# Packing a 96-token expert down product into column groups: 64 latent tokens on two groups of 64, 32 context tokens on four groups of 32

## The chip, the cores and the metric

The kernel runs on one core of one Trainium2 chip. The metric is device time in microseconds (us) of one launch; lower is better. TensorE multiplies a stationary operand (up to 128 rows by 128 columns, loaded by a weight load) with a moving operand that streams through it, and accumulates in PSUM, a memory of 128 partitions in 8 banks. All data are 32-bit floats, and each matmul of the program shows in the trace as two records with a weight load each.

## The reference

Two layers act on 256 context tokens and 512 latent tokens of width 1024. Each has a token mixer (four branches) and then a mixture of 16 experts, in which each expert chooses its tokens. Only the experts matter here:

```python
def ec_moe(h, w_router, w_e_gate, w_e_up, w_e_down):
    b, t, d = h.shape
    cap = EC_CAPACITY * t // N_EXPERTS
    aff = jax.nn.softmax((h @ w_router).astype(jnp.float32), axis=-1)
    vals, idx = lax.top_k(jnp.swapaxes(aff, 1, 2), cap)
    xs = jax.vmap(lambda hb, ib: hb[ib])(h, idx)
    hid = jax.nn.silu(jnp.einsum('becd,edf->becf', xs, w_e_gate)) * jnp.einsum('becd,edf->becf', xs, w_e_up)
    ys = jnp.einsum('becf,efd->becd', hid, w_e_down) * vals[..., None].astype(h.dtype)
    return jax.vmap(lambda yb, ib: jnp.zeros((t, d), yb.dtype).at[ib.reshape(-1)].add(yb.reshape(-1, d)))(ys, idx)
```

Latent and context tokens are chosen apart: an expert takes 64 latent tokens, and in the first layer also 32 context tokens (the second layer's context output isn't needed). The hidden width is 1408 (11 blocks of 128).

## The kernel before

Each engine has a program of its own; semaphores order them. `moe(L)` on each engine runs the expert stage of layer L as a loop over 16 experts (15 in the loop, the last one after it). `cap` is 96 in the first layer and 64 in the second; `two` is true in the second layer only.

*Weights.* SP streams an expert's weights in nine pieces of at most 2 MiB through three slots of the tile `ring`: gate 0, up 0, gate 1, up 1, gate 2, up 2 (the last two 384 columns wide, 1.5 MiB), then three pieces of the down weights (4, 4 and 3 blocks of 128 rows). A slot is refilled (`freed`, `piece`, issues at L2314 and L2319) when TensorE has used the piece that lies in it, so a piece is asked for three pieces ahead.

*TensorE, for each expert.* `gate_up(0)`; `choose()` for the next expert (L959, and L963 in the second layer): products of a 0/1 selection `e_sel` with the token numbers and affinities `e_ta`, which give the next expert's row offsets and scales; `gate_up(1)`; `gate_up(2)`; `turn_rows()` (L972), which transposes the next expert's gathered rows; then `down(0)`, `down(1)`, `down(2)` (L1026), which begin after the previous expert's results have been taken out of PSUM (`ys_a`, `ys_d`). In the first layer `gate_up` (L999) makes the hidden values in transposed form, 64 weight columns on each of two column groups and the 96 tokens moving. `down` has the tokens' hidden values `e_hidT` stationary and the down weights moving: two matmuls of 512 columns for each of the 11 blocks k. In the second layer the two halves of the output go to PSUM partitions 0 to 63 and 64 to 127, so that each uses its own group of 64 columns of the array. In the first layer all 96 tokens are stationary, and both halves write partitions 0 to 95.

```python
for half in range(2):
    lo = 64 * half if two else 0
    ins = pe.matmul(banks[6 + half][lo:lo + cap, :], e_hidT[:, at, 0:cap], w[:, k, half * 512:half * 512 + 512],
                    start=(f == 0), stop=(f == NF - 1))
```

*The others.* ScalarE takes out the first output half (times the affinity, from `s_sel`) into `e_ys`, VectorE the second (L1535). GpSimd then scatters `e_ys` into the rows `f_rows` in memory (`scatter`, L2198), adding, and before that gathers the next expert's rows (`gather`, L2189) with the offsets `idx` that VectorE copies from what `choose` made (`next_chosen`, `now_chosen`, L1540).

Elsewhere, the modulation product `ada_rows` (L537) puts block k on column group k mod 4, with 32 stationary columns each.

Of the kernel before, what the change touches and what calls it, by code (L numbers as in the profile page):

```python
# [19 lines left out]
ALU = mybir.AluOpType  # L20
AF = mybir.ActivationFunctionType
AX = mybir.AxisListType
P = 128
# [5 lines left out]
NT = T // P  # L29
# [127 lines left out]
def hybrid_layers(nc, I, out, stop=None):  # L157
    ctx = ExitStack()
    with ctx:
# [266 lines left out]
        s_pc = small[:, 492:504].rearrange("p (i t) -> p i t", i=2)  # L426
        s_mrow = area(WORK_W - 1024, 1024).rearrange("p (b n) -> p b n", b=2)
        s_l = small[:, 512:640]
        s_sel = small[:, 504:506]

        def parts(n, cap):

# [14 lines left out]
        def _(pe):  # L447
# [486 lines left out]
            def moe(L):  # L934
# [20 lines left out]
                def choose():  # L955

                    pe.wait_ge(sems["sel"], c.nth("sel"))
                    for t in QT:
                        ins = pe.matmul(banks[5][0:cap, 0:2], e_sel[:, t, 0:cap], e_ta[:, t, :], start=(t == QT[0]), stop=(t == QT[-1]))  # L959
                    if two:  # L960

                        for t in QT:
                            ins = pe.matmul(banks[5][64:64 + cap, 0:2], e_sel[:, t, 0:cap], e_ta[:, t, :],  # L963
                                            start=(t == QT[0]), stop=(t == QT[-1]))
                    ins.then_inc(sems["chosen"], 1)

                def turn_rows():
# [8 lines left out]
                def expert(e, last):  # L976
                    def wpiece(i):
                        n = n0 + i
                        pe.wait_ge(sems[f"w_in{n % SLOTS}"], (e * 3 + (n // SLOTS + 1)) * 16)

                    def gate_up(g):

                        for u in range(2):
                            wpiece(2 * g + u)
                            n = EXP_W[2 * g + u]
                            w = slot(n0 + 2 * g + u, n)
                            for k in range(KD if two else 0):

                                b = banks[(0, 2, 0)[g] + u]
                                pe.matmul(b[0:64, 0:256], e_xs[:, k, 0:64], w[:, k, 0:256], start=(k == 0), stop=(k == KD - 1))  # L990
                                ins = pe.matmul(b[64:128, 0:n - 256], e_xs[:, k, 0:64], w[:, k, 256:n],  # L991
                                                start=(k == 0), stop=(k == KD - 1))
                            for f in range(0 if two else n // P):

                                b = banks[(0, 2, 0)[g] + u]
                                for k in range(KD):
                                    for half in range(2):
                                        lo, c0 = 64 * half, f * P + 64 * half
                                        ins = pe.matmul(b[lo:lo + 64, f * cap:(f + 1) * cap], w[:, k, c0:c0 + 64], e_xs[:, k, 0:cap],  # L999
                                                        start=(k == 0), stop=(k == KD - 1))  # L1000
                            ins.then_inc(sems["gu"], 1)

                    def turn_hidden(g):

                        pe.wait_ge(sems["hid"], c.nth("hid"))
                        pe.nop(nofuse=True)
                        b = banks[(4, 5, 4)[g]]
                        for j in range(2 if two else 0):

                            rows = P if 4 * g + 2 + j < NF else 64  # L1010
                            ins = pe.transpose(b[:, j * P:j * P + rows], e_hid[0:rows, 512 * g + j * P:512 * g + (j + 1) * P],
                                               ident[0:rows, 0:rows])
                        ins.then_inc(sems["hid_t"], 1)

                    def down(i):
                        if two or i == 2:
                            pe.wait_ge(sems["hid_f"], c.nth("hid_f"))
                        wpiece(6 + i)
                        kk = EXP_DOWN[i]
                        w = slot(n0 + 6 + i, 1024, kk)  # L1020
                        for k in range(kk):
                            f = 4 * i + k
                            at = 4 * i + ((0, 2, 1, 3)[k] if two else k)
                            for half in range(2):
                                lo = 64 * half if two else 0
                                ins = pe.matmul(banks[6 + half][lo:lo + cap, :], e_hidT[:, at, 0:cap], w[:, k, half * 512:half * 512 + 512],  # L1026
                                                start=(f == 0), stop=(f == NF - 1))
                        ins.then_inc(sems["ys"], 1)

                    pe.wait_ge(sems["xs"], c.nth("xs"))  # L1030
                    gate_up(0)
                    if not last:
                        choose()
                    gate_up(1)
                    if two:
                        turn_hidden(0)
                    else:
                        pe.wait_ge(sems["hid_f"], c.nth("hid_f"))
                    gate_up(2)
                    if not last:  # L1040

                        pe.wait_ge(sems["idx_next"], c.nth("idx_next"))
                    if two:
                        turn_hidden(1)
                    else:
                        pe.wait_ge(sems["hid_f"], c.nth("hid_f"))
                    if not last:
                        turn_rows()

                    pe.wait_ge(sems["ys_a"], c.nth("ys_a"))  # L1050
                    pe.wait_ge(sems["ys_d"], c.nth("ys_d"))
                    down(0)
                    if two:
                        turn_hidden(2)
                    down(1)
                    down(2)

# [45 lines left out]
        def _(act):  # L1103
# [3 lines left out]
            def do(*a, **kw):  # L1107
                c.seq(act.activation(*a, **kw))  # L1108
# [318 lines left out]
            def moe(L):  # L1427
# [23 lines left out]
                def expert():  # L1451
                    hidden(0)
                    hidden(1)
                    if cap == 64:
                        turned(0)
                    hidden(2)
                    if cap == 64:
                        turned(1)
                        turned(2)

                    act.wait_ge(sems["idx_now"], c.nth("idx_now"))
                    act.wait_ge(sems["ys"], c.nth("ys", 3))
                    do(e_ys[0:cap, 0:512], banks[6][0:cap, :], AF.Copy, scale=s_sel[0:cap, 1:2])
                    act.sem_inc(sems["ys_a"], 1)

                act.sem_inc(sems["ys_a"], 1)
                per = {"gu": 6, "idx_now": 1, "ys": 3, "act_order": 4 + 4 * (cap == 64)} | ({"hid_t": 3} if cap == 64 else {})
                with act.Fori(0, NE) as e:
                    c.begin(e, per)
                    expert()  # L1470
# [51 lines left out]
        def _(dve):  # L1522
# [16 lines left out]
            def copy(o_, a):  # L1539
                S(dve.tensor_copy(o_, a))  # L1540
# [496 lines left out]
            def moe(L):  # L2037
# [2 lines left out]
                S(dve.memset(e_sel, 0.0))  # L2040
                ts(e_ta[:, :, 0], cc("tokens"), -float(first_row[L]), ALU.add)
                cap = CAPS if len(QS) == 2 else CAP_L
                both = P if cap == 64 else cap

                def select(e):

                    copy(s_pc[:, 0, t0:NT], e_pos[:, t0:NT, bass.ds(e, 1)].squeeze(2))
# [8 lines left out]
                def next_chosen():  # L2056

                    dve.wait_ge(sems["chosen"], c.nth("chosen"))
                    copy(idx[0:cap, 0:1], banks[5][0:cap, 0:1])
                    copy(s_sel[0:both, 0:1], banks[5][0:both, 1:2])  # L2060
                    dve.sem_inc(sems["idx_next"], 1)

                def now_chosen():
                    copy(idx[0:cap, 1:2], idx[0:cap, 0:1])
                    copy(s_sel[0:both, 1:2], s_sel[0:both, 0:1])
                    dve.sem_inc(sems["idx_now"], 1)

                def tokens():
# [28 lines left out]
                def expert(e, last):  # L2097
                    if not last:
                        select(e + 1)
                    hidden(0)  # L2100
                    dve.wait_ge(sems["put"], c.nth("put"))
                    now_chosen()
                    if not last:
                        next_chosen()
                    hidden(1)
                    hidden(2)
                    if not last:
                        tokens()
                    dve.wait_ge(sems["ys"], c.nth("ys", 3))
                    ts(e_ys[0:cap, 512:1024], banks[7][both - cap:both, :], s_sel[both - cap:both, 1:2], ALU.mult)  # L2110
                    dve.sem_inc(sems["ys_d"], 1)

                select(0)
# [1 line left out]
                tokens()  # L2115
                dve.sem_inc(sems["ys_d"], 1)
                per = {"silu": 3, "gu": 6, "chosen": 1, "rows_t": 1, "ys": 3, "put": 1,
                       "dve_order": 2 + len(QS) + 2 + 3 + (cap == 64) + 3 * len(QS) + 1 + 2}
                with dve.Fori(0, NE - 1) as e:
                    c.begin(e, per)  # L2120
                    expert(e, False)
# [360 lines left out]
```

## Time and profile before

| | |
|---|---|
| median of 3 runs | 3922.82 us (3918.15 to 3925.51) |
| span of the profiled execution, first to last instruction | 3927.2 us (no separate time of it was recorded) |
| first layer's expert stage | from 1341 us to about 2162 us |
| second layer's expert stage | from 3211 us to about 3900 us |
| TensorE busy in all | 3615.3 us, 92% of the span |
| mean granted TensorE clock | 0.958 of full speed |

The profile comes from one execution. PE is TensorE's matmuls, PEld its weight loads, DVE VectorE, ACT ScalarE, POOL GpSimd, SP the engine that issues the weight DMAs. Matmuls are pipelined, so a record lasts longer than the step from one to the next: steps are read from starts.

### The profile page before, as it was taken

Reading aid. Unit: us, or ns where it says so; the run is one execution under the profiler, and the core shown is the slowest. Engines: PE = TensorE matmul, PEld = TensorE weight load, DVE = VectorE, ACT = ScalarE, POOL = GpSimd, SP = SyncE. Lnnn points to the kernel's source line nnn. Section 1 sums busy time; section 2 is a strip of 40 time slices with the busy share of each in tenths; the row PEclk is TensorE's granted clock in tenths of the full one; section 3 lists DMA queues with packets and bytes.
Section 4 is the critical chain, followed back from the end, with each engine's and each line's share of the span. In section 5 each row is a group of like instructions: output and inputs, shape, how many; then the busy total and the mean of one; then the engine's idle time right before and its main releaser. Section 6 shows DMA issues by size and latency. Waiting matters only on the chain.

```text
span 3927.2 us, 63160 instructions
## 1 busy us (share of the span) xinstructions
PE 3615.3 (92%) x26440; PEld 2513.5 (64%) x26440; DVE 1091.0 (28%) x2410; ACT 702.6 (18%) x1331; POOL 127.7 (3%) x184
## 2 busy tenths in 40 slices
PE   6999999999999999999999999998989998888886
PEld 3565766767785877777777766756677664444443
DVE  0333323426612411111110452315165231111111
ACT  3322312012213000000000332221122211101101
POOL 0000100000000000000000000000000000000000
PEclk9999999999899999999999999898989999999998
DMA  5662010020102499999999202020111239999997
GB/s 203 229 227 72 22 54 22 12 75 28 56 25 85 150 348 356 354 356 348 353 356 345 90 28 71 23 75 11 54 37 61 75 150 412 412 411 414 414 410 315
DMA packets 121756, 740.26 MB, mean 188 GB/s; under 512 B 7808, under 2 KB 13952, under 8 KB 84624
## 3 DMA queue, kind: packets, MB, share of 16 engines
q1 hardware_dynamic: 110000, 695.29, 45.2%
q0 software_dynamic: 11616, 43.05, 3.8%
q8 instruction: 95, 1.56, 0.2%
q14 instruction: 45, 0.37, 0.0%
HBM read 713.09 MB, written 25.21 MB: 188 GB/s over the span
## 4 chain that ended last, share of the span: by engine, by line
PE 75%; DMA 15%; DVE 5%; ACT 3%; issue 1%; DVEq 0%; SPq 0%; POOL 0%; ACTq 0%; POOLq 0%
PE psum L566 13%; PE psum L1026 10%; PE psum L999 9%; PE psum L494 7%; DMA ring<-in_w_e_gate 6%; DMA ring<-in_w_e_down 6%; PE psum L487 5%; PE psum L471 4%; PE psum L990 4%; PE psum L892 4%; PE psum L568 3%; PE psum L656 3%; PE psum L674 2%; PE psum L761 2%; DMA ring<-in_w_e_up 2%; DVE work L1531 2%
## 5 line engine op out<-in xcount | busy, mean ns | idle before, releaser
L566 PE MATMUL psum<-HT,ring 128*128 128x256 f32 x2560 | 624.3, 400 | 17.9 <-DVEq L1607 7.8
L566 PEld LDWEIGHTS psum<-HT,ring 128*128 128x128 f32 x2560 | 509.4, 202 | 121.8 <-issue 29.2
L1026 PE MATMUL psum<-ring,work 128*96 128x512 f32 (+1 forms) x1408 | 466.3, 596 | 24.7 <-DMA ring<-in_w_e_down 24.6
L999 PE MATMUL psum<-work,ring 128*64 128x96 f32 x11264 | 474.9, 246 | 6.3 <-issue 4.2
L999 PEld LDWEIGHTS psum<-work,ring 128*64 128x64 f32 x11264 | 466.4, 137 | 21.4 <-issue 18.0
L990 PE MATMUL psum<-ring,work 128*64 128x256 f32 x1536 | 371.1, 399 | 97.8 <-DMA ring<-in_w_e_gate 73.4
L990 PEld LDWEIGHTS psum<-ring,work 128*64 128x64 f32 x1536 | 212.9, 143 | 230.7 <-DMA ring<-in_w_e_gate 89.0
L991 PE MATMUL psum<-ring,work 128*64 128x256 f32 (+1 forms) x1536 | 352.0, 369 | 0.0
L1026 PEld LDWEIGHTS psum<-ring,work 128*96 128x96 f32 (+1 forms) x1408 | 166.2, 150 | 289.7 <-issue 256.9
L494 PE MATMUL psum<-ring,HT 128*128 128x512 f32 (+1 forms) x768 | 276.0, 521 | 0.0
L1108 ACT ACTIVATE work<-psum,small 128x768 f32<-128x768 f32 (+3 forms) x176 | 131.2, 745 | 784.0 <-PE psum L1026 493.8
L494 PEld LDWEIGHTS psum<-ring,HT 128*128 128x128 f32 x768 | 145.8, 190 | 127.2 <-issue 120.5
L1111 ACT ACTIVATE work<-psum 128x512 f32<-128x512 f32 (+8 forms) x229 | 109.9, 480 | 629.9 <-PE psum L494 236.9
L487 PE MATMUL psum<-HT,ring 128*128 128x512 f32 (+5 forms) x624 | 216.0, 508 | 6.5 <-ACTq L1174 6.2
L991 PEld LDWEIGHTS psum<-ring,work 128*64 128x64 f32 x1536 | 194.9, 142 | 1.0
L1108 ACT ACTIVATE YT<-psum,pack 128x256 f32<-128x256 f32 x160 | 75.9, 474 | 616.2 <-PE psum L568 569.3
L1535 DVE TENSOR_SCALAR work<-psum,small 128x64 f32<-128x64 f32 (+3 forms) x122 | 52.9, 434 | 479.4 <-PE psum L1026 432.0
L487 PEld LDWEIGHTS psum<-HT,ring 128*128 128x128 f32 (+2 forms) x624 | 112.5, 182 | 108.1 <-issue 91.9
L1108 ACT ACTIVATE X<-psum 128x384 f32<-128x384 f32 (+3 forms) x112 | 43.4, 387 | 757.7 <-PE psum L999 420.2
L471 PE MATMUL psum<-const 128*128 128x256 f32 x732 | 170.1, 391 | 0.0
L568 PE MATMUL psum<-YT 128*128 128x256 f32 x640 | 164.3, 379 | 0.0
L471 PEld LDWEIGHTS psum<-const 128*128 128x128 f32 x732 | 142.4, 197 | 19.9
(172 smaller groups left out, 3253.2 us busy)
## 6 DMA issues: line engine op xcount, KB each, us to landing
ring<-in_w_e_gate SPq DMA_DIRECT2D x64, 2048.0 KB, 9.5
ring<-in_w_e_up SPq DMA_DIRECT2D x64, 2048.0 KB, 10.4
ring<-in_w_e_down SPq DMA_DIRECT2D x64, 2048.0 KB, 9.7
ring<-in_w_ada SPq DMA_DIRECT2D x24, 2048.0 KB, 9.5
ring<-in_w_e_gate SPq DMA_DIRECT2D x32, 1536.0 KB, 12.1
ring<-in_w_e_up SPq DMA_DIRECT2D x32, 1536.0 KB, 8.9
ring<-in_w_e_down SPq DMA_DIRECT2D x32, 1536.0 KB, 9.7
ring<-in_w_gate SPq DMA_DIRECT2D x16, 2048.0 KB, 8.9
```

The source lines that it names most:

```text
L471: pe.matmul(b[:, 0:256], ident, const[:, 0:256], start=True, stop=True)
L487: ins = pe.matmul(b[0:M, 0:n], w[:, k, c0:c0 + M], HT[:, k, off:off + n], start=(k == 0), stop=(k == KD - 1))
L494: ins = pe.matmul(b[:, 0:n], HT[:, k, t * P:(t + 1) * P], w[:, k, c0:c0 + n], start=(k == 0), stop=(k == KD - 1))
L566: pe.matmul(b[:, 0:256], w[:, k, d4 * P:(d4 + 1) * P], HT[:, k, off:off + 256], start=(k == 0), stop=(k == KD - 1))
L568: ins = pe.matmul(b[:, 256:512], wbr[:, m % 2, i, d4 * P:(d4 + 1) * P], YT[:, n_ % 2, i, off:off + 256], start=(i == 0), stop=(i == 1))
L656: ins = pe.matmul(b[:, m, at:at + ln], q(it, m), k(it, m, at, ln), start=True, stop=True)
L892: ins = pe.matmul(b[:, :], mT[:, k, t * P:(t + 1) * P], w[:, k, :], start=(k == 0), stop=(k == KD - 1))
L990: pe.matmul(b[0:64, 0:256], e_xs[:, k, 0:64], w[:, k, 0:256], start=(k == 0), stop=(k == KD - 1))
L991: ins = pe.matmul(b[64:128, 0:n - 256], e_xs[:, k, 0:64], w[:, k, 256:n], start=(k == 0), stop=(k == KD - 1))
L999: ins = pe.matmul(b[lo:lo + 64, f * cap:(f + 1) * cap], w[:, k, c0:c0 + 64], e_xs[:, k, 0:cap], start=(k == 0), stop=(k == KD - 1))
L1026: ins = pe.matmul(banks[6 + half][lo:lo + cap, :], e_hidT[:, at, 0:cap], w[:, k, half * 512:half * 512 + 512], start=(f == 0), stop=(f == ...
L1108: c.seq(act.activation(*a, **kw))
```

## The change

In the first layer the down product is made in two loops for each piece of weights. The first has the 64 latent tokens stationary, one output half on each of two 64-column groups, as the second layer does. The second has the 32 context tokens stationary, each quarter of the output (256 columns) on one of four 32-column groups, into bank 4. `choose` therefore makes offsets and scales for latent tokens on two partition ranges and for context tokens on four; `s_sel` has a column for each kind. The evictions become one of 64x512 and two of 32x256 for ScalarE and the same for VectorE. The second layer's products are the same as before, except that `choose` alternates the two groups from tile to tile (one loop in place of two).

```diff
                 def choose():
                     pe.wait_ge(sems["sel"], c.nth("sel"))
-                    for t in QT:
-                        ins = pe.matmul(banks[5][0:cap, 0:2], e_sel[:, t, 0:cap], e_ta[:, t, :], start=(t == QT[0]), stop=(t == QT[-1]))
-                    if two:
-                        for t in QT:
-                            ins = pe.matmul(banks[5][64:64 + cap, 0:2], e_sel[:, t, 0:cap], e_ta[:, t, :],
-                                            start=(t == QT[0]), stop=(t == QT[-1]))
+                    for t in range(CT, NT):
+                        for lo in (0, 64):
+                            ins = pe.matmul(banks[5][lo:lo + CAP_L, 0:2], e_sel[:, t, 0:CAP_L], e_ta[:, t, :],
+                                            start=(t == CT), stop=(t == NT - 1))
+                    for t in range(0 if two else CT):
+                        for q in range(4):
+                            ins = pe.matmul(banks[5][32 * q:32 * q + CAP_C, 2:4], e_sel[:, t, CAP_L:CAPS], e_ta[:, t, :],
+                                            start=(t == 0), stop=(t == CT - 1))
                     ins.then_inc(sems["chosen"], 1)
...
                             for half in range(2):
-                                lo = 64 * half if two else 0
-                                ins = pe.matmul(banks[6 + half][lo:lo + cap, :], e_hidT[:, at, 0:cap], w[:, k, half * 512:half * 512 + 512],
-                                                start=(f == 0), stop=(f == NF - 1))
+                                lo = 64 * half
+                                ins = pe.matmul(banks[6 + half][lo:lo + CAP_L, :], e_hidT[:, at, 0:CAP_L],
+                                                w[:, k, half * 512:half * 512 + 512], start=(f == 0), stop=(f == NF - 1))
+                        for k in range(0 if two else kk):
+                            f = 4 * i + k
+                            for q in range(4):
+                                ins = pe.matmul(banks[4][32 * q:32 * q + CAP_C, 0:256], e_hidT[:, f, CAP_L:CAPS],
+                                                w[:, k, q * 256:q * 256 + 256], start=(f == 0), stop=(f == NF - 1))
                         ins.then_inc(sems["ys"], 1)
...
-                    do(e_ys[0:cap, 0:512], banks[6][0:cap, :], AF.Copy, scale=s_sel[0:cap, 1:2])
+                    do(e_ys[0:CAP_L, 0:512], banks[6][0:CAP_L, :], AF.Copy, scale=s_sel[0:CAP_L, 1, 0:1])
+                    for q in range(2 if cap != 64 else 0):
+                        do(e_ys[CAP_L:CAPS, 256 * q:256 * q + 256], banks[4][32 * q:32 * q + CAP_C, 0:256], AF.Copy,
+                           scale=s_sel[32 * q:32 * q + CAP_C, 1, 1:2])
...
-                    copy(idx[0:cap, 0:1], banks[5][0:cap, 0:1])
-                    copy(s_sel[0:both, 0:1], banks[5][0:both, 1:2])
+                    copy(idx[0:CAP_L, 0:1], banks[5][0:CAP_L, 0:1])
+                    if cap != 64:
+                        copy(idx[CAP_L:CAPS, 0:1], banks[5][CAP_L:CAPS, 2:3])
+                        copy(s_sel[:, 0, :], banks[5][:, 0:4].rearrange("p (g c) -> p g c", g=2)[:, :, 1])
+                    else:
+                        copy(s_sel[:, 0, 0:1], banks[5][:, 1:2])
...
-                    ts(e_ys[0:cap, 512:1024], banks[7][both - cap:both, :], s_sel[both - cap:both, 1:2], ALU.mult)
+                    ts(e_ys[0:CAP_L, 512:1024], banks[7][64:64 + CAP_L, :], s_sel[64:64 + CAP_L, 1, 0:1], ALU.mult)
+                    for q in range(2, 4 if cap != 64 else 2):
+                        ts(e_ys[CAP_L:CAPS, 256 * q:256 * q + 256], banks[4][32 * q:32 * q + CAP_C, 0:256],
+                           s_sel[32 * q:32 * q + CAP_C, 1, 1:2], ALU.mult)
```

## Rows read from the trace of the kernel before

**Rows 1.** The page: its span, and DMA busy tenths in 40 slices.
```profile
span 3927.2 us, 63160 instructions
...
DMA  5662010020102499999999202020111239999997
```

**Rows 2.** Stages: us, busy us (instructions) per engine, PE clock, DMA share, GB/s.
```profile
1341.00:2145.00 804.00, 790.89 (x12233) 601.00 (x12234) 99.54 (x276) 51.80 (x78) 35.73 (x30) 1.00 0.93 350
3211.00:3900.00 689.00, 570.87 (x4233) 320.11 (x4232) 80.21 (x237) 68.82 (x143) 35.93 (x31) 0.97 0.99 404
```

**Rows 3.** Timeline of one expert, TensorE: start us, us, what, count [idle before].
```profile
1607.79 1.18 PE L959 MATMUL psum<-X 128*96 128x2 f32 x12
1608.90 18.88 PE L999 MATMUL psum<-work,ring 128*64 128x96 f32 x448
...
1629.69 19.09 PE L1026 MATMUL psum<-ring,work 128*96 128x512 f32 x44 [1.10 <-DMA ring<-in_w_e_down]
...
1630.60 0.16 PEld L1026 LDWEIGHTS psum<-ring,work 128*96 128x96 f32 x1 [0.27 <-issue]
...
1647.76 0.16 PEld L1026 LDWEIGHTS psum<-ring,work 128*96 128x96 f32 x1 [0.27 <-issue]
...
1648.71 1.46 PE L999 MATMUL psum<-work,ring 128*64 128x96 f32 x30
```

**Rows 4.** Timeline of the modulation product, four groups of 32 columns.
```profile
143.86 1.92 PE L537 MATMUL psum<-ring,small 128*32 128x512 f32 x16
145.72 1.05 PE L546 MATMUL psum<-const,work 128*128 128x2 f32 x8
```

**Rows 5.** Timeline of the second layer's down product, first piece, two groups.
```profile
3238.71 3.65 PE L1026 MATMUL psum<-ring,work 128*64 128x512 f32 x16
3242.30 0.53 PE L1011 MATMUL psum<-const,X 128*128 128x128 f32 x2
```

**Rows 6.** Waits from 1341 to 2145 us: total us, times, longest.
```profile
PE psum L1026 <- DMA ring<-in_w_e_down: 6.9, 9, 1.2
```

**Rows 7.** Chain that ended last, 1590 to 1720 us: start us, us, what.
```profile
1671.36 9.55 DMA ring<-in_w_e_down
...
1681.05 19.09 PE psum L1026 x44
```

**Rows 8.** DMA issues of 1636.9 to 1637.4 us: KB, us to landing.
```profile
ring<-in_w_e_gate SPq DMA_DIRECT2D x1, 2048.0 KB, 7.7
```

**Rows 9.** DMA issues from 1341 to 2145 us: KB each, median us to landing.
```profile
ring<-in_w_e_down SPq DMA_DIRECT2D x32, 2048.0 KB, 9.1
ring<-in_w_e_up SPq DMA_DIRECT2D x31, 2048.0 KB, 11.1
...
X<-xn_rows,idx POOLq DMA_INDIRECT x15, 7.9
f_rows<-work,idx POOLq DMA_INDIRECT x15, 11.6
```

**Rows 10.** The same from 3211 to 3900 us.
```profile
ring<-in_w_e_down SPq DMA_DIRECT2D x32, 2048.0 KB, 9.7
ring<-in_w_e_up SPq DMA_DIRECT2D x31, 2048.0 KB, 10.0
ring<-in_w_e_gate SPq DMA_DIRECT2D x30, 2048.0 KB, 9.5
ring<-in_w_e_gate SPq DMA_DIRECT2D x16, 1536.0 KB, 12.1
...
f_rows<-work,idx POOLq DMA_INDIRECT x16, 9.3
```

**Rows 11.** A group by form: count, busy us, mean ns, idle before.
```profile
L1108 ACT ACTIVATE YT<-psum,pack 128x256 f32<-128x256 f32 x160 | 75.9, 474 | 616.2 <-PE psum L568 569.3 <-DVEq L1607 44.4 <-ACT YT L1108 1.3
```

**Rows 12.** Timeline, next expert's gather and when its rows are turned.
```profile
1663.93 0.94 POOL L2189 DMA_INDIRECT X<-xn_rows,idx  x1 [11.98 <-DVEq L2061]
...
1679.16 0.70 PEld L972 LDWEIGHTS psum<-const,X 96*128 96x128 f32 x8
```

More of the change, by code:

```diff
@@ L428, in hybrid_layers @@
         s_l = small[:, 512:640]
-        s_sel = small[:, 504:506]
+        s_sel = small[:, 504:508].rearrange("p (i g) -> p i g", i=2)
         def parts(n, cap):
@@ L1462, in expert @@
                     act.wait_ge(sems["ys"], c.nth("ys", 3))
-                    do(e_ys[0:cap, 0:512], banks[6][0:cap, :], AF.Copy, scale=s_sel[0:cap, 1:2])
+                    do(e_ys[0:CAP_L, 0:512], banks[6][0:CAP_L, :], AF.Copy, scale=s_sel[0:CAP_L, 1, 0:1])
+                    for q in range(2 if cap != 64 else 0):
+                        do(e_ys[CAP_L:CAPS, 256 * q:256 * q + 256], banks[4][32 * q:32 * q + CAP_C, 0:256], AF.Copy,
+                           scale=s_sel[32 * q:32 * q + CAP_C, 1, 1:2])
                     act.sem_inc(sems["ys_a"], 1)
                 act.sem_inc(sems["ys_a"], 1)
-                per = {"gu": 6, "idx_now": 1, "ys": 3, "act_order": 4 + 4 * (cap == 64)} | ({"hid_t": 3} if cap == 64 else {})
+                per = {"gu": 6, "idx_now": 1, "ys": 3, "act_order": 8 if cap == 64 else 6} | ({"hid_t": 3} if cap == 64 else {})
                 with act.Fori(0, NE) as e:
@@ L2042, in moe @@
                 cap = CAPS if len(QS) == 2 else CAP_L
-                both = P if cap == 64 else cap
                 def select(e):
@@ L2064, in now_chosen @@
                     copy(idx[0:cap, 1:2], idx[0:cap, 0:1])
-                    copy(s_sel[0:both, 1:2], s_sel[0:both, 0:1])
+                    copy(s_sel[:, 1, 0:1 + (cap != 64)], s_sel[:, 0, 0:1 + (cap != 64)])
                     dve.sem_inc(sems["idx_now"], 1)
@@ L2117, in moe @@
                 per = {"silu": 3, "gu": 6, "chosen": 1, "rows_t": 1, "ys": 3, "put": 1,
-                       "dve_order": 2 + len(QS) + 2 + 3 + (cap == 64) + 3 * len(QS) + 1 + 2}
+                       "dve_order": 2 + len(QS) + 2 + 3 + (cap == 64) + 3 * len(QS) + 1 + 2 + 3 * (cap != 64)}
                 with dve.Fori(0, NE - 1) as e:
```

## Prediction

> **What bounds the kernel now.** I read the page first: its second part shows the DMA engines nine tenths busy in two stretches only [rows 1]. They are the expert stages, the first layer's from 1341 us on and the second's from 3211 us. The table by stage tells them apart [rows 2]: in the first TensorE is busy 790.89 of 804.00 us while the DMA moves 350 GB/s; in the second the DMA share is 0.99 at 404 GB/s and TensorE is busy 570.87 of 689 us. The first stage, the only one whose down product is changed, is bound by TensorE, with DMA close behind.
>
> Next, TensorE's own order within one expert [rows 3]. Gate and up are pairs of 64-column products (L999, 42 ns a record: 18.88 us for 448). The choice for the next expert (L959) takes 1.11 us. Then the gathered rows are turned (L972), and the down product (L1026) takes 44 records, 22 matmuls in two passes each, from 1629.69 to 1648.71: 19.02 us. From one down product to the next are 51.36 us [rows 3, 7], so it is 37% of an expert. Its weight loads start every 0.429 us (1630.60 to 1647.76 is 40 steps): that is the time in which 512 columns stream, whether the stationary operand has 96 columns or fewer.
>
> The table of waits says how much DMA already costs there: 6.9 us in nine waits before L1026, on down pieces [rows 6], or 0.4 per expert. VectorE, ScalarE and GpSimd wait for TensorE.
>
> **The change, part by part.** Per expert and per contraction block k (11 of them):
>
> Latent tokens. Before, the two output halves follow one another with 96 columns each: 4 records, 1.716 us. After, each half is on its own group of 64 columns. The second layer's down product has just this form: 16 records of 512 columns take 3.59 us until the next instruction starts [rows 5], 8 x 0.429 = 3.43 plus 0.16. So two run at once and a k costs 0.858 us; 11 cost 9.44.
>
> Context tokens. Four matmuls of 32 columns, 256 wide, one per group. The nearest row is the modulation product L537: four groups of 32, 512 wide. Its 16 records take 1.86 us until the next form starts [rows 4], 4 x 0.429 = 1.72 plus 0.14, although here too both passes of one matmul are issued before the next group's. So four run at once, and 256 columns should take half: 2 x 0.2145 = 0.429 us a k, 4.72 for 11. That 256 columns take half of 512 is from the stream's length; L999's 96 columns at 84 ns a pair bear it out (0.429 x 96/512 = 80 ns).
>
> Streaming: 44 x 0.429 = 18.88 before, 9.44 + 4.72 = 14.16 after: **-4.72 us** per expert. With groups that ran only two at a time the context part would cost 9.44 and the gain would be gone; that is the worse bound, below as a rival.
>
> Changes of form. The array's layout now changes inside each of the three pieces (64 to 32) and back between them, and at the end: six blocks where one stood, five more. The three blocks above cost 0.14, 0.16 and 0.14 us beyond their steps (for L1026, 19.02 - 18.88), start and change together, so **+0.73 us** (5 x 0.145). The lower bound is 0 if these hide, the upper is in the next paragraph.
>
> The row shows that L999 starts at 1648.71, 0.07 us before the last record of L1026 ends at 1648.78 [rows 3]. The Trainium skill's page TensorEngine Tiling (Array Packing), Key Properties, says that a change of tiling mode drains the engine. By the rows the five changes make 0.73; if each waited for the last record to end (0.64 - 0.43 = 0.21, the 0.64 being 19.09 - 43 x 0.429) and then for a weight load (0.16), they would make 5 x 0.37 = 1.85. I take the rows' value and keep the other as a rival.
>
> Choosing (L959). Twelve records of 96 columns, one after the other, take 1.11 us. They become 16 of 64 columns that alternate between two groups and 16 of 32 columns over four. L999's records on two groups step at 42 ns [rows 3]: 0.67 us for the first 16, and between half of that and as much for the others. One more change of form costs 0.15, and the entry, now of L999's own form, saves as much. Together 1.0 to 1.35 us: I take **0** (bounds -0.1 and +0.25). In the second layer the same 16 records alternate now; with DMA the limit there [rows 2] this is nothing.
>
> Evictions. ScalarE and VectorE had one of 512 columns each and now have one of 512 and two of 256; the nearest row of 256 columns is 0.474 us [rows 11], so they end some 0.9 to 1.0 us later. Queued behind are, on VectorE, the choice for the next expert (needed 11 us later) and on GpSimd the scatter. The scatter starts 0.9 us later, so the row offsets and then the gather may do so: the gather is issued at 1663.93 and lands after 7.9 us in the median [rows 9], TensorE turns its rows only at 1679.16, so 7 us of cover are left [rows 12]; the wait of TensorE for these evictions is passed before the next down product, 30 us on. Nothing per expert; uncovered once, at the stage's end: **+1 us**. The two more small copies in the choice lie in the same 7 us. Were that cover gone, each tenth would cost 1.6 us in all.
>
> Waits on DMA. SP refills a slot of the three when TensorE has used the piece in it, so each piece is asked for three pieces ahead. The first down piece of the shown expert is asked for at 1671.36 and lands 9.55 us later, its product starts at 1681.05, with 1.0 us of waiting before it [rows 7]; [rows 3] show 1.10 for the expert before. That wait stays: what lies between asking and need (two short pieces and the turn) isn't changed. But down pieces are used in 5.4 us rather than 6.86 (4 k x 1.29 + 0.29), so the next gate, up and gate pieces are asked for more densely. The first gate piece, asked for last of a sparse stretch, lands after 7.7 us [rows 8], the pieces in general after 9.1 to 11.1 [rows 9]; the next expert's first gate piece will be wanted 5.4 + 4.1 = 9.5 us after it is asked for, up from 11.8. It would just land. I take **+0.4 us** per expert, as much again as today; bounds 0 and the rival's.
>
> Sum per expert: -4.72 + 0.73 + 0.4 = -3.59. For 16 experts -57.4, plus 1 at the end: **-56.4 us**. The profiled execution spans 3927.2 us [rows 1], 4.4 above the median of the runs (3922.8) and 1.7 above their highest; against the span the sum gives 3870.8, against the median 3866.4 us. I forecast the median: **3866 us**. The second layer's code and data path aren't touched and simply move earlier.
>
> **Rivals.**
> - *DMA takes over.* Stage one moves 350 GB/s; an expert shorter by 3.6 of 51.4 us needs 376, and the second stage reaches 404 [rows 2]. So mean rate isn't the limit, but the three slots could be. If each landing takes as long as in the second layer [rows 10], the slot that holds gate, up and down needs 9.5 + 5.4 + 10.0 + 5.4 + 9.7 + 5.4 = 45.4 us per expert, and the one with up, short gate (12.1) and down 10.0 + 5.4 + 12.1 + 4.0 + 9.7 + 5.4 = 46.6. A 96-row scatter lands 2.3 us later than a 64-row one (11.6 against 9.3) [rows 9, 10]: 47.7 to 48.9 per expert. The mean now is some 50.8: the 51.36 of the expert shown, with its wait of 1.0 put at the mean of 0.4. Gain 1.9 to 3.1 us per expert, 30 to 50 us: **3873 to 3893**. For it: landings already set the down product's start. Against: today's landings in the first stage aren't all as slow (down 9.1, gate 7.7 to 9.1).
> - *A change of form drains the array.* +1.12 us per expert, +18: **3884**. Against it stand all three blocks' 0.14 to 0.16 [rows 3 to 5]. (This is what the page's rule would do.)
> - *The context groups run two at a time* (the other side). The context part costs 9.44 instead of 4.72, +75 us: **3942**, slower by 19. It decides from a k step of 0.75 us on (0.429 + 3.53/11). Place: the second loop of the down product. For it: the same group's two passes are issued back to back. Against: L537 has the same order and ran four at once [rows 4].
> - *Better than forecast*: waits vanish and changes hide, -4.7 us per expert: down to 3847.
>
> **How the numbers follow.** Forecast 0.60 (its own range 3853 to 3877, from changes at 0.5 to 1.0 and waits at 0 to 1.0 us per expert); DMA 0.25; drain 0.06; two at a time 0.03; better 0.04; 0.02 for something not seen that gives back nearly all. The range 3849 to 3891 takes in forecast, DMA and drain and leaves out under 2 in 10. The bound of 0.2% is 8 us, about what a measurement of this kernel can tell from no change: faster 0.95, same 0.02, slower 0.03.
>
> **What would show it.** The latent loop should show 64-column records two per 0.429 us; the context loop 32-column records four per 0.21 us; a down product 15 us long with six blocks; an expert's period near 47.2 us; the granted clock at 1.00, the level of 2.4 GHz, as now [rows 2]; waits on gate pieces at L999 of a few tenths per expert. The prediction is wrong if a context k takes over 0.5 us, if the blocks cost over 0.25 us each, or if waits on DMA in this stage pass 25 us in all (16 experts at 0.4 + 1.2).

## The result, and the profile after

| | before | after |
|---|---|---|
| median | 3922.82 us (3918.15 to 3925.51, 3 runs) | 4035.73 us (4028.44 to 4038.79, 4 runs) |
| ratio to before | | 1.0287, 95% interval 1.0269 to 1.0306 |
| span of the profiled execution | 3927.2 us | 4026.7 us |

A fourth execution of the kernel before took 6193.34 us and is left out, of the ratio too. The change makes the kernel 2.9% slower, 113 us by the medians, where 3866 us had been forecast. The page after, its span and the lines of its second part:

```profile
span 4026.7 us, 66773 instructions
...
PEclk8999999989899998899889999898989999999998
DMA  5652010110112588888888600110011229999997
```

In [rows 1] the first of the two dense stretches of DMA showed nines; now it shows eights. The first stage as a whole, and three windows of it, the middle one the idle time after a down product and the last the first gate and up pieces that follow. Columns as in [rows 2]:

```profile
1341.00:2260.00 919.00, 774.66 (x13989) 612.25 (x13991) 119.08 (x326) 65.72 (x108) 35.75 (x30) 0.92 0.84 312
1614.00:1624.30 10.30, 10.23 (x96) 3.58 (x88) 0.00 (x0) 0.00 (x1) 0.00 (x0) 1.00 0.99 388
1624.30:1629.20 4.90, 0.00 (x0) 0.00 (x0) 2.75 (x7) 2.89 (x4) 1.44 (x1) 0.90 1.02 354
1629.20:1646.70 17.50, 13.09 (x256) 12.79 (x258) 0.00 (x0) 0.49 (x1) 0.00 (x0) 0.74 0.57 186
```

TensorE is now idle for 144 of the stage's 919 us, against 13 of 804 [rows 2]: it does less work, in more time. The timeline of one expert, TensorE alone, shows where:

```profile
1609.11 3.65 PE L1027 MATMUL psum<-ring,work 128*64 128x512 f32 x16
1612.69 1.93 PE L1032 MATMUL psum<-ring,work 128*32 128x256 f32 x32
...
1620.00 2.79 PE L1027 MATMUL psum<-ring,work 128*64 128x512 f32 x12
1622.73 1.50 PE L1032 MATMUL psum<-ring,work 128*32 128x256 f32 x24
1629.21 1.53 PE L1000 MATMUL psum<-work,ring 128*64 128x96 f32 x14 [4.98 <-issue]
1635.15 11.72 PE L1000 MATMUL psum<-work,ring 128*64 128x96 f32 x241 [4.41 <-issue]
...
1646.71 0.65 PE L960 MATMUL psum<-X 128*64 128x2 f32 x15
1647.29 0.31 PE L964 MATMUL psum<-X 128*32 128x2 f32 x16
1647.53 18.70 PE L1000 MATMUL psum<-work,ring 128*64 128x96 f32 x448
1666.16 0.88 PE L973 MATMUL psum<-const,X 96*128 96x96 f32 x8
1667.10 3.65 PE L1027 MATMUL psum<-ring,work 128*64 128x512 f32 x16
```

The down product is what was forecast. Its first latent block takes 3.58 us until the next starts, its first context block 1.86 (1612.69 to 1614.55, where the next latent block starts). From 1609.11 to the end of the last record at 1624.23 are 15.12 us, against 19.02 from start to start [rows 3]. But then, at the head of the next pass of TensorE's loop, it stands for 4.98 us, makes 14 records and stands for 4.41 us more, with "issue" as the reason: it waits for no semaphore that the profile shows. The table of waits of the stage (1341 to 2260 us):

```profile
PE psum L1000 <- issue: 135.4, 30, 5.7
...
PE psum L1027 <- DMA ring<-in_w_e_down: 6.5, 9, 1.2
```

30 waits, about two for each of the 14 branches back (15 passes), 135 us in all. The down pieces' landing costs what it cost [rows 6]. The row that names the cause is a small one, the queue that brings instructions. Over the first stage, before (1341 to 2145 us):

```profile
q8 instruction: 12, 0.20, 0.1%
```

and after (1341 to 2260 us; packets, MB, share of the engines' time):

```profile
q8 instruction: 140, 2.29, 1.0%
```

The trace gives each fetch its time: between one branch back of TensorE's loop and the next lie 9 of them in every pass, where the trace before has none. One pass of the loop has 876 records of products in the trace after (704 + 44 + 88 + 32 + 8), each with a weight load, and 15 instructions of the sequencer: 1767. Before it had 768 records and 1551 instructions. 2.29 MB in 140 are 16.4 KB a fetch; if an instruction takes 64 bytes, which the moved loops below put to the test, that is a block of 256 instructions.

### The profile page after: what moved, and what is told of

It reads as the page before. It is cut to its first block, busy times and chain, and to the rows that moved or that the text cites. A ratio compares the mean times of both kernels' runs of the same rounds, so it can differ in the third digit from the quotient of the medians.

```text
span 4026.7 us, 66773 instructions
## 1 busy us (share of the span) xinstructions
PE 3579.5 (89%) x28168; PEld 2519.0 (63%) x28168; DVE 1109.9 (28%) x2458; ACT 717.5 (18%) x1363; POOL 127.8 (3%) x184
## 4 chain that ended last, share of the span: by engine, by line
PE 72%; DMA 15%; DVE 5%; issue 5%; ACT 3%; DVEq 0%; SPq 0%; POOL 0%; ACTq 0%; POOLq 0%
PE psum L566 12%; PE psum L1000 10%; PE psum L494 7%; DMA ring<-in_w_e_down 6%; PE psum L1027 6%; DMA ring<-in_w_e_gate 6%; PE psum L487 5%; PE psum L471 4%; PE psum L892 3%; PE psum L991 3%; PE psum L568 3%; PE psum L656 2%; PE psum L674 2%; PE psum L1032 2%; PE psum L501 2%
## 5 line engine op out<-in xcount | busy, mean ns | idle before, releaser
L1000 PE MATMUL psum<-work,ring 128*64 128x96 f32 x11264 | 509.8, 255 | 137.4 <-issue 135.4
L1000 PEld LDWEIGHTS psum<-work,ring 128*64 128x64 f32 x11264 | 498.9, 144 | 150.3 <-issue 148.6
L991 PEld LDWEIGHTS psum<-ring,work 128*64 128x64 f32 x1536 | 212.0, 143 | 234.2 <-DMA ring<-in_w_e_gate 90.1
L1027 PE MATMUL psum<-ring,work 128*64 128x512 f32 x1408 | 322.5, 598 | 26.9 <-DMA ring<-in_w_e_down 26.5
L1114 ACT ACTIVATE work<-psum,small 128x768 f32<-128x768 f32 (+3 forms) x208 | 146.0, 702 | 720.2 <-PE psum L1032 319.2
L1027 PEld LDWEIGHTS psum<-ring,work 128*64 128x64 f32 x1408 | 101.9, 136 | 197.5 <-issue 163.3
L992 PEld LDWEIGHTS psum<-ring,work 128*64 128x64 f32 x1536 | 194.3, 142 | 0.0
L1544 DVE TENSOR_SCALAR work<-psum,small 128x64 f32<-128x64 f32 (+2 forms) x154 | 68.6, 446 | 421.8 <-PE psum L1032 207.9
L1540 DVE TENSOR_TENSOR work<-X,psum 128x384 f32<-128x384 f32 (+1 forms) x48 | 25.0, 521 | 557.2 <-PE psum L1000 557.2
## 6 DMA issues: line engine op xcount, KB each, us to landing
ring<-in_w_e_gate SPq DMA_DIRECT2D x32, 1536.0 KB, 10.5
```

Of the source, the lines that this page charges most:

```text
L1027: ins = pe.matmul(banks[6 + half][lo:lo + CAP_L, :], e_hidT[:, at, 0:CAP_L], w[:, k, half * 512:half * 512 + 512], start=(f == 0), stop=(f ...
```

## The experiments

Two theories stood. **Code fetch:** TensorE keeps 8 such blocks (the theory's own premise); the new loop touches 8 and one more is read ahead, so all of them are fetched anew in each pass, and a pass waits for its first blocks. **The array:** going from four groups of 32 columns back to two of 64, or the new use of bank 4, stalls the next expert. A third, that the weight slots are refilled too late, was weak already, since the waits are not put down to DMA and only "issue" grew.

All kernels below that start with a_ have the changed products in full. Slot n means that the loop's first instruction is the nth (from 0) of a fetch block. The edit, in TensorE's program (`L == 0` is the first layer):

```diff
-                with pe.Fori(0, NE - 1) as e:
+                eng = [pe.engine]
+                with (nc.Fori(0, NE - 1, engines=bass.OrderedEngineSet(eng), head_slot={pe.engine: 0}) if L == 0 else pe.Fori(0, NE - 1)) as e:
```

**The changed kernel at slot 0.**

> The changed kernel; TensorE's loop over the first layer's experts is laid so that its first instruction is the first of a 256-instruction fetch block. Nothing else differs. Code-fetch theory (the loop of 1767 TensorE instructions fills 7 blocks and touches 8 where it now lies, one more is read ahead, and 9 don't stay resident, so every iteration fetches all of them again and waits at its first two): laid at slot 0 it touches 7, fetches during the loop vanish, the two waits of about 5 us per iteration vanish, and the time is 3866 us or up to 15 above, faster than before by 1.1 to 1.5%. Rival (the array going from four groups of 32 to two of 64, or bank 4, stalls the next expert): nothing changes, 4030 to 4040 us. Rival (the weight slots are refilled too late): nothing changes.

Measured: 3870.09 us, ratio 0.9858 (0.9839 to 0.9876); a second time, 3876.29 us, ratio 0.9883 (0.9864 to 0.9902), 2 us above what was expected of the second. The first one's timeline at the same place:

```profile
1623.26 2.79 PE L1027 MATMUL psum<-ring,work 128*64 128x512 f32 x12
1625.99 1.50 PE L1032 MATMUL psum<-ring,work 128*32 128x256 f32 x24
1627.42 10.99 PE L1000 MATMUL psum<-work,ring 128*64 128x96 f32 x256
1638.24 0.58 PE L960 MATMUL psum<-X 128*64 128x2 f32 x16
1638.75 0.31 PE L964 MATMUL psum<-X 128*32 128x2 f32 x16
1639.44 5.79 PE L1000 MATMUL psum<-work,ring 128*64 128x96 f32 x130 [0.39 <-DMA ring<-in_w_e_gate]
```

and from its tables of queues and waits over 1341 to 2150 us:

```profile
q8 instruction: 15, 0.25, 0.1%
```
```profile
PE psum L1000 <- DMA ring<-in_w_e_up: 8.4, 16, 1.0
PE psum L1000 <- DMA ring<-in_w_e_gate: 8.3, 19, 0.9
...
PE psum L1000 <- issue: 3.1, 4, 1.3
PE psum L1027 <- DMA ring<-in_w_e_down: 1.9, 2, 1.3
```

The same products, in the same order, from four groups of 32 to two of 64: 1.43 us after the last context block starts, L1000 starts, with no wait. The down product takes 15.05 us from start (1612.37) to start. The theory of the array falls with this run alone, and so does that of the weight slots, whose refills the edit leaves as they are.

> The changed kernel at slot 0 once more, beside the one with the turned order: 3866 to 3874 us.

**The limit.** Slots 16, 32 and 48 differ in the edit by that number only. The last column counts the whole execution; the kernel before has 95, the kernel as changed 222.

> The changed kernel with the loop laid at slot 16: 16 + 1767 = 1783, under 7 blocks (1792). Code-fetch theory: as at slot 0, 3862 to 3878 us, no fetches in the loop. If only an exact block start helped: about 3975 or more.

> The changed kernel with the loop laid at slot 32: 32 + 1767 = 1799, 7 instructions over 7 blocks. Code-fetch theory: 9 fetches per iteration again and one wait of 5 us, as at slot 48, 3970 to 3985 us. If the limit lies higher than reckoned: 3870.

> The same with the loop's first instruction at slot 48 of a fetch block: 48 + 1767 = 1815 instructions is just over 7 blocks (1792), so 8 are touched. Code-fetch theory: as slow as the changed kernel, 4025 to 4045 us, with 9 fetches of 16 KB per iteration. If only a fixed waste at the old place had counted (any shift helps), 3866 to 3880 us. Rivals of the array or the weight slots: 4030 to 4040 us too, so this one speaks only together with slot 0.

| slot | slot + 1767 | us | ratio (interval) | q8 fetches in all |
|---|---|---|---|---|
| 0 | 1767 | 3870.09 | 0.9858 (0.9839 to 0.9876) | 96 |
| 16 | 1783 | 3874.20 (2 runs) | 0.9876 (0.9844 to 0.9908) | 96 |
| 32 | 1799 | 3973.40 (2 runs) | 1.0129 (1.0098 to 1.0159) | 223 |
| 48 | 1815 | 3975.41 | 1.0135 (1.0114 to 1.0156) | 223 |

The pages of slots 16 and 32 have

```profile
q8 instruction: 96, 1.57, 0.2%
```
```profile
q8 instruction: 223, 3.65, 0.4%
```

and 99 us lie between them. So the limit is between 1783 and 1799, and 7 blocks are 1792; past it come 127 fetches more, 9 for each of the 14 branches back. Slot 48 was expected at 4025 to 4045 us and missed this by 50 us. Its fetches are all there, but a pass has only one long wait, at the loop's head (5.0 to 5.4 us, beside small ones of up to 1.3):

```profile
1613.53 12.68 PE L1000 MATMUL psum<-work,ring 128*64 128x96 f32 x256 [5.34 <-issue]
```

In the kernel as changed the head lies some 30 instructions ahead of a block's end (14 products with their loads, and a few of the sequencer), so the second block is wanted at once and waited for too; here 208 instructions come first and hide nearly all of its fetch. I take that for the reason why the same change can cost 113 or some 50 us; slot 32, with 224 instructions to its first boundary, agrees. After the wait the 256 records take 12.68 us instead of the 10.78 of the stage's first expert, at a mean granted clock of 0.84; in the kernel as changed the window that follows the waits has a mean granted clock of 0.74, between the levels of 1.2 and 2.4 GHz, where the busy window before them has 1.00 (table by window above).

**A hint for the branch back.** The edit adds `hint_back_edge=True` to the loop and sets no slot.

> The changed kernel with a prefetch hint for TensorE's branch back at the top of each iteration. Code-fetch theory: the wait for the branch's target goes (about 5 us of the 9.4 idle per iteration), the wait for the block behind it may stay: 3960 us, anywhere from 3880 to 4000. Rivals of the array or the weight slots: 4030 to 4040.

Measured: 3881.00 us, 0.9893 (0.9875 to 0.9911), at the lower end of the 3880 to 4000 us expected, 79 us under the middle value. Its queue of instructions shows why:

```profile
q8 instruction: 16, 0.26, 0.1%
```

I had thought that only the branch's target would come early. Instead no block is fetched at all during the loop. The trace has one more TensorE instruction in each pass, the hint (1768), and the loop's head lies where it lay, to one instruction, so the loop still touches 8 blocks, and 8 blocks can stay. With nine fetches a pass where nothing is done, that fits 8 kept blocks with the ninth, read ahead for nothing, as the one too many: I infer that the hint puts the target in its place. No run shows that separately.

**The loop written out.** (Abridged: what follows `else` is the old loop, for the second layer.)

```diff
-                with pe.Fori(0, NE - 1) as e:
-                    c.begin(e, per)
-                    expert(e, False)
...
+                if L == 0:
+                    for e in range(NE - 1):
+                        expert(e, False)
+                else:
...
```

> The changed kernel with TensorE's loop over the first layer's experts written out 16 times instead of branching back. Code-fetch theory: blocks are fetched in order ahead of use, no wait at an expert's start, 3866 to 3885 us, with about 7 fetches per expert. Rival of the array: 4030 to 4040 us, since the order of products is the same. Rival of the weight slots: the same 4030 to 4040.

Measured: 3917.22 us, 0.9984 (0.9968 to 0.9999). It removes the long waits (so the array's theory falls again), but 47 us of the gain are missing. Waits and queue, 1341 to 2150 us:

```profile
PE psum L1000 <- issue: 45.1, 46, 2.2
```
```profile
q8 instruction: 110, 1.80, 0.9%
```

It was expected at 3866 to 3885 us. Blocks fetched in order come late too, by up to 2.2 us, beside weight DMAs that keep the engines nine tenths busy. My assumption that reading in order is hidden was wrong here: resident code is worth 47 us (3917 - 3870).

**Does the old product stall as well, if its loop is too long?** The kernel before, with padding at the loop's end, at slots 0 and 239.

```diff
+                    for _ in range(8 if L == 0 else 0):
+                        pe.nop(nofuse=True)
```

> The kernel before, with 8 empty instructions at the end of TensorE's loop over the first layer's experts (1559 in all) and the loop laid at slot 0 of a fetch block. Code-fetch theory: 7 blocks are touched as before, nothing is fetched in the loop; the empty instructions cost some tenths of a us per expert at most: 3920 to 3932 us. It is the control for the next one.

> The same kernel, 8 empty instructions and the old down product on 96 columns, with the loop laid at slot 239: 239 + 1559 = 1798 instructions, 8 blocks touched. Code-fetch theory: it becomes slow without any packing, about 9 fetches and two waits of 4 to 5 us per iteration (the first block boundary comes 17 instructions after the loop's head), 4040 to 4090 us. Rival (the packed form of the down product causes the stall, and the place of the loop only moves it): 3920 to 3935 us.

Measured: 3917.67 us, 0.9982 (0.9968 to 0.9996), 2 us under what was expected, and 3920.29 us, 0.9995 (0.9982 to 1.0008). The second missed its expectation for a plain reason: the trace has 1551 instructions a pass, the empty ones were dropped, and 239 + 1551 = 1790 is inside the limit. So it is a fair point below the limit and no test above it. Then with real padding:

```diff
+                    for _ in range(2 if L == 0 else 0):
+                        pe.matmul(banks[4][:, 0:2], ident, const[:, 0:2], start=True, stop=True)
```

> The compiler dropped the 8 empty instructions of the last pair: its loop had 1551 and at slot 239 ended at 1790, 2 under the limit of 1792. Here two products of two columns into the unused bank 4 stand in their place, 8 real instructions (1559 in all), at slot 0. Extra work: the two products, 0.2 to 0.6 us per iteration. Code-fetch theory: no fetches in the loop, 3920 to 3934 us.

> The same kernel, down product on 96 columns as before the change, at slot 239: 239 + 1559 = 1798, 6 over the limit. Code-fetch theory: about 9 fetches and two waits of 4 to 5 us per iteration, 4030 to 4090 us, with none of the packed products in it. Rival (only the packed form can stall): 3920 to 3934 us, as at slot 0.

Measured: 3928.22 us, 1.0017 (1.0003 to 1.0031), and 3998.07 us, 1.0197 (1.0171 to 1.0223). The same instructions, 70 us apart by where they lie, with the unpacked down product of before. At slot 239, timeline and queue:

```profile
1620.38 0.54 PE L999 MATMUL psum<-work,ring 128*64 128x96 f32 x7
1624.11 11.99 PE L999 MATMUL psum<-work,ring 128*64 128x96 f32 x249 [3.19 <-issue]
```
```profile
q8 instruction: 121, 1.98, 1.0%
```

At slot 0 the queue has 11, and the same place of the timeline is

```profile
1647.58 0.50 PE L1069 MATMUL psum<-const 128*128 128x2 f32 x4
1648.02 10.78 PE L999 MATMUL psum<-work,ring 128*64 128x96 f32 x256
```

So the packed form isn't needed for the stall, and the limit lies between 1790 and 1798. The size was forecast too high (4030 to 4090 us): a pass loses 5 us (70 over 14) instead of 9. It stands at the next boundary, 7 records in, for 2.4 to 3.5 us, and never at the head. The head is fetched all the same: the trace has nine fetches per branch back here too (117 more than at slot 0; one of the 14 has none and no wait, why is open), one of them some 1 us behind the branch, which I take for the head's. It is covered. By the sequencer's records the branch lies 6.3 us ahead of the next L999, at slot 0 as at slot 239, since the slow products of L1026 are still being worked off. In the packed loop at slot 0 it is 1.3 us in most passes; in the kernel as changed, where the head has to be fetched, 6.3 to 7.0. No run varies this distance by itself.

**Fewer changes of form.** The changed kernel at slot 0, context before latent in the second down piece:

```diff
+                        elif i == 1:
+                            context()
+                            ins = latent()
```

(Abridged: `latent` and `context` hold the two loops of a piece, which the other pieces run in the old order.)

> The changed kernel at slot 0, with the order of latent and context products turned round in the second of the three down pieces, so that two of the six blocks' changes of form go. By the 0.15 us that a block costs, 0.3 us per expert, 4.7 us in all, if it is on the path: 3865 us. If the weights' landings now set the pace (rival), nothing: 3870 us.

Measured: 3872.06 us, 0.9877 (0.9855 to 0.9900), beside 0.9883 (0.9864 to 0.9902) for slot 0 in the same comparison. The intervals lie on each other: inconclusive. The trace has the longer blocks,

```profile
1615.25 3.66 PE L1037 MATMUL psum<-ring,work 128*32 128x256 f32 x64
1618.84 6.23 PE L1028 MATMUL psum<-ring,work 128*64 128x512 f32 x28
```

the two pairs 3.59 us and 6.16 us to the next start, 0.16 and 0.15 above 16 x 0.2145 and 14 x 0.429, so two changes are gone; but its waits for gate and up pieces are 10.9 and 9.2 us in all instead of 8.3 and 8.4, and for down pieces 2.9 instead of 1.9: 4.4 us more, where 4.7 were to be saved. What TensorE saves, it waits, as the expectation's rival had it; but the second trace of slot 0 has as much waiting (23.0 us), so this is likely and not shown.

## Why the prediction was wrong

The terms, set against the kernel at slot 0, which has every part of the change and none of the fetches:

- *Streaming*, right: latent blocks two records per 0.429 us, context blocks four per 0.2145. 16 and 32 records take 3.58 and 1.86 us, 3.43 and 1.72 plus 0.15 and 0.14.
- *Changes of form*, right: 0.14 to 0.15 us per block, not the 0.37 of the rival. On the Trainium skill's rule of a drain (TensorEngine Tiling (Array Packing), Key Properties): these rows leave no room for waiting out a record and then a load.
- *Choosing*, too high: from 1638.24 to L1000's start at 1639.44 are 1.20 us, 0.39 of it a wait for the gate piece, so 0.8, a gain of 0.3 against the 1.11 before, where 0 was taken; this lies outside the term's bound of -0.1.
- *Evictions*, right: nothing per expert, TensorE waits for neither. Once at the stage's end, the wait before the next product (L931) is 5.15 us instead of 4.06: the +1 of the forecast.
- *Waits on DMA*, too small: 8.4 + 8.3 + 1.9 = 18.6 us for gate, up and down pieces, 1.2 per expert, and 23.0 us, 1.4 per expert, in the trace of the second measurement of slot 0. Before they are 8.0 (6.9 on down pieces and 1.1 on the others), or 0.5; that is +0.7 and +0.9 instead of +0.4. They moved from the down pieces to gate and up pieces.
- *The sum*: 3870 and 3876 us measured, 3866 forecast. In the traces the stage, from the first L999 or L1000 to L931, is 823.0 us before and 769.7 and 778.3 at slot 0, 53 and 45 shorter where 56.4 were forecast. The terms as measured make 56 and 52, so 3 and 7 us have no name.

What failed is the step that made this sum the whole of the change, "Sum per expert: -4.72 + 0.73 + 0.4 = -3.59". It left out that 216 more TensorE instructions per pass have to be held, and that a loop too long for that has to be brought from memory in each pass. I had counted their records for time (32 in place of 12 in the choice, 132 in place of 44 in the down product) and never for code size, and so the fetch queue of the kernel before, 12 fetches in a stage of 15 passes, was not read for what it says: that the loop of 1551 instructions stayed resident. None of the four rivals held it either, and none of the three signs of being wrong came at slot 0 (a context k takes 1.86/4 = 0.47 us, a block costs 0.15, waits stay under 25). A slip in the sums is small beside this: the forecast's own range, given as 3853 to 3877, is 3856 to 3880 by its terms. The missing term: 9.4 us of waiting per branch back (4.98 + 4.41), some 2 us of slower products after it, less 1 us of DMA waits that it covers. 14 x 10.5 = 147 us; the trace has 921.1 us from the first L1000 to L931 and 769.7 at slot 0, 151 apart, of 153 between the two profiled executions.

The two rivals of the array are out: neither drain nor two-at-a-time shows in any block. The rival that DMA takes over is not out. It gave 3873 to 3893 us, and the second 3876 lies in it; the waits have doubled and more, and the turned order above won nothing clear of the noise. For what the products save, 3866 was a little too good.

The Trainium skill's page Runtime: NRT & Kernel Launch, Instruction fetch mechanics, says that TensorE's instruction memory holds 128 KiB, 2048 instructions, refilled in 16 KiB blocks of 256. This case agrees: fetches of 16.4 KB, 8 blocks that can stay, a limit at 7 with one read ahead. It also says that a taken branch whose target isn't in the current window of 2 pages waits for its fetch. The wait of 5 us at the target agrees; the window of 2 does not, since at slot 0 TensorE branches back over 7 blocks 14 times without a fetch. The same section calls the cost of crossing into the next block mostly hidden; the loop written out measured 45 us of it, so here the measurement decides.

## What to carry to other kernels

Packing small products into column groups gave what its rows promised, but trades stream time for instructions: count those of a loop's body as a cost of their own. Where the count nears 7 blocks of 256 on TensorE, the place of the loop's head decides: 4% of this kernel between as changed and slot 0. So read the instruction queue's fetches against the number of passes, and set the head or the hint. The best version run here is the change with its loop at slot 0: 1.2 to 1.4% faster than before.

## What was not expected of the hardware

A fetch of one 16 KB block is waited for 4.9 to 5.7 us at the branch's target in the kernel as changed, and 3.9 to 4.8 at the block behind it, beside the weight DMAs, though the packet itself takes 1.0 us in the median of the stage. In the written-out loop TensorE waited 46 times for code, by up to 2.2 us: at 42 ns for a record with its load, 256 instructions last 5.4 us, hardly longer than such a fetch is waited for. The hint for the branch back stopped the fetches of all blocks, not of one. Place alone (same instructions) was worth 166 us for the packed loop, as changed against slot 0, and 70 us for the other. Where the old, slower products lie before the branch, the fetch at its target cost nothing that shows: the branch ran 6.3 us ahead of the first product behind it, as without any fetch.
